# Pass change and last products of a down stage, and one turn in the attention stage: order and pages changed

## The reference, cut to what matters

```
u = rmsnorm(x);  proj = u @ w_in
ya, yb, yc = three attentions (A: 4 heads with two maps each; C: 8 heads; B: 8 heads, windowed)
h = x + rmsnorm((sum of sigmoid(gates) * (y @ w_proj)) @ w_out)
u = rmsnorm(h)
act = gelu(conv(u @ w_ffn_up)[:, :2816]) * conv(...)[:, 2816:]
out = h + rmsnorm(act @ w_ffn_down)          # 512x2816 @ 2816x1024
```

## Time and profile before

| | |
|---|---|
| median of 3 runs | 871.23 us |
| profiled execution's own time | 870.49 us |
| its span, first to last instruction | 868.7 us |
| mean granted TensorE clock | 0.995 |
| TensorE busy | 851.2 us, 98% |
| VectorE / ScalarE / GpSimd busy | 519.0 / 430.5 / 394.0 us |
| HBM read / written | 91.81 / 8.17 MB |

### The profile page before, as it was taken

The page is one execution under the profiler, slowest core; times in us unless marked ns, Lnnn a source line. Parts: engine busy times, 40 slices in busy tenths (PEclk is TensorE's granted clock), DMA queues, the critical chain, the costliest instruction groups (busy, mean ns, idle before and its releaser), DMA issues.

```text
span 868.7 us, 12772 instructions
## 1 busy us (share of the span) xinstructions
PE 851.2 (98%) x4182; PEld 715.1 (82%) x4182; DVE 519.0 (60%) x1050; ACT 430.5 (50%) x775; POOL 394.0 (45%) x542
## 2 busy tenths in 40 slices
PE   9999999999999999999999999999999999999877
PEld 7888887888888888888888889888888888888765
DVE  5677887888766733222222366555555555898884
ACT  6566666877666743333322526444444443454552
POOL 4554443234344447666666747555555554000001
PEclk9999999999999999999999999999999999999998
DMA  7541232322232223332328343333333333256472
GB/s 216 159 122 55 80 86 70 95 73 79 79 80 79 62 82 89 109 97 85 109 97 264 100 146 115 115 115 115 115 115 115 115 115 115 73 182 200 146 252 117
DMA packets 137617, 100.57 MB, mean 116 GB/s; under 512 B 7431, under 2 KB 122063, under 8 KB 137572
## 3 DMA queue, kind: packets, MB, share of 16 engines
q1 hardware_dynamic: 136666, 96.81, 36.6%
q10 hardware_dynamic: 906, 3.20, 1.0%
HBM read 91.81 MB, written 8.17 MB: 115 GB/s over the span
## 4 chain that ended last, share of the span: by engine, by line
PE 91%; DVE 4%; DMA 2%; issue 1%; POOL 1%; ACT 1%; SPq 1%; DVEq 0%; POOLq 0%; ACTq 0%
PE banks L1667 27%; PE banks L1669 26%; PE banks L1668 26%; PE banks L1838 2%; PE banks L1746 2%; PE banks L1747 2%; PE banks L1810 1%; DMA scratch<-second_tokens 1%; DMA ring_raw<-in_w_in_dram 1%; PE banks L1817 1%; DVE ring_lo L1593 1%; PE banks L1801 1%; DVE pages L1601 1%; PE banks L2016 1%; DVE scratch L1466 1%
## 5 line engine op out<-in xcount | busy, mean ns | idle before, releaser
L706 POOL TENSOR_TENSOR ring_lo<-ring_raw,ring_hi 128x256 fp32r<-128x256 f32 x472 | 357.9, 790 | 313.3 <-ACT ring_hi L818 313.2
L1667 PE MATMUL banks<-u_hi,ring_hi 128*128 128x512 f32 (+1 forms) x768 | 300.4, 391 | 0.2 <-DVE u_lo L1171 0.2
L1669 PE MATMUL banks<-u_hi,ring_lo 128*128 128x512 f32 (+1 forms) x768 | 296.0, 385 | 0.0
L1668 PE MATMUL banks<-u_lo,ring_hi 128*128 128x512 f32 (+1 forms) x768 | 295.6, 385 | 0.0
L1669 PEld LDWEIGHTS banks<-u_hi,ring_lo 128*128 128x128 f32 x768 | 144.3, 188 | 29.3
L1667 PEld LDWEIGHTS banks<-u_hi,ring_hi 128*128 128x128 f32 x768 | 144.4, 188 | 27.6 <-DVE u_lo L1171 0.4
L1668 PEld LDWEIGHTS banks<-u_lo,ring_hi 128*128 128x128 f32 x768 | 144.5, 188 | 27.3
L818 ACT CAST ring_hi<-ring_raw 128x1024 fp32r<-128x1024 f32 x118 | 122.8, 1043 | 61.2 <-PE banks L1669 54.2
L1507 DVE SCALAR_TENSOR_TENSOR wide<-banks,cols,wide 128x511 f32<-128x511 f32 x88 | 65.9, 749 | 96.4 <-ACT wide L1074 90.9
L1074 ACT ACTIVATE wide<-banks,cols 128x512 f32<-128x512 f32 x44 | 34.3, 778 | 98.0 <-PE banks L1669 98.0
L722 POOL TENSOR_SCALAR norm_ms<-norm_ss 128x1 f32<-128x1 f32 x15 | 2.9, 190 | 135.2 <-ACT pages L828 134.9
(11 more groups left out here) (217 smaller groups left out, 1337.3 us busy)
## 6 DMA issues: line engine op xcount, KB each, us to landing
ring_raw<-in_w_ffn_up_dram SPq DMA_DIRECT2D x88, 256.0 KB, 3.3
ring_raw<-in_w_in_dram SPq DMA_DIRECT2D x60, 256.0 KB, 3.4
ring_raw<-in_w_ffn_down_dram SPq DMA_DIRECT2D x55, 256.0 KB, 3.4
ring_raw<-in_w_gate_dram SPq DMA_DIRECT2D x48, 256.0 KB, 3.1
ring_raw<-in_w_out_dram SPq DMA_DIRECT2D x16, 256.0 KB, 2.9
second_tokens<-wide SPq DMA_DIRECT2D x10, 384.0 KB, 3.8
scratch<-second_tokens SPq DMA_DIRECT2D x10, 384.0 KB, 4.4
scratch<-in_x_dram SPq DMA_DIRECT2D x4, 512.0 KB, 5.9
```

What stands on the lines that cost most here:

```text
L706: last = pool.tensor_tensor(wlo[:, r, c], raw[:, r, c], whi[:, r, c].bitcast(F32), ALU.subtract)
L1667: pe.matmul(out, lhs_hi, rhs_hi, start=start, stop=False)
L1668: pe.matmul(out, lhs_hi, rhs_lo, start=False, stop=False)
L1669: return pe.matmul(out, lhs_lo, rhs_hi, start=False, stop=stop)
```

## The change

Four constants and orders change, in four places:

- `BY_TILE` 4 to 3 and `BY_PRODUCT` 3 to 2. In the last m, m3 of half 0 follows m2 of half 0 for each m.
- e21 of the two halves goes to pages of its own, `wide[:, 1, :]` and `scratch[:, 0, :]` (the first t4 page, free after its split). Both `make_e21` stand together, ahead of both `add_m5`. `split_second(1)` moves ahead of them on VectorE, and ahead of the copies back on ScalarE.
- SyncE issues the gain and all four residual rows after the last weight row and second tokens, gain first, then tiles 0, 2, 3, 1 (2 and 3 with a wait for `act2_lo` 9 and 10).
- In slot 18 `turn_y(3)` comes before the last projection step, and VectorE's `y_low_a(3)` before `results(17)`.

```diff
--- before.py
+++ after.py
@@ -67,7 +67,7 @@
 LAST_PAIR_AT = 6
 DOWN_SLOTS = (2, 3, 0)
 DOWN_ORDER = (0, 2, 3, 1)
-BY_TILE, BY_PRODUCT = 4, 3
+BY_TILE, BY_PRODUCT = 3, 2
 N_PAGES = 2 * FT
 
 SC_BANK, PT_BANK, O_BANK, G_BANK = 0, 2, 4, 6
@@ -302,7 +302,7 @@
         def kept_part(t):
             return raw[:, 1, 512 * t:512 * t + 512]
 
-        spare_part = wide[:, 1, :]
+        e21_parts = (wide[:, 1, :], scratch[:, 0, :])
         g_post_2 = xs_tmp
         spare_tmp = wide[:, 0:2, :].rearrange("p h n -> p (h n)")
 
@@ -671,13 +671,12 @@
                 load_down(FH + 3 + m)
                 if m + 2 < FH - 1:
                     load_second(m + 2)
-                if m == 6:
-                    sp.wait_ge(t4_lo, 7)
-                    for t in (0, 1):
-                        sp.dma_start(x_tok[:, t, :], h_dram[t]).then_inc(h_again[t], 16)
-                    sp.dma_start(g_post_2, g_post_ffn[0].partition_broadcast(P)).then_inc(gain_ffn_loaded, 16)
-            sp.wait_ge(act2_lo, FH - 1)
-            for t in (2, 3):
+            sp.wait_ge(t4_lo, 7)
+            sp.wait_ge(e21_back, 2)
+            sp.dma_start(g_post_2, g_post_ffn[0].partition_broadcast(P)).then_inc(gain_ffn_loaded, 16)
+            for t in DOWN_ORDER:
+                if t >= 2:
+                    sp.wait_ge(act2_lo, FH + t - 4)
                 sp.dma_start(x_tok[:, t, :], h_dram[t]).then_inc(h_again[t], 16)
             for i, t in enumerate(DOWN_ORDER[:-1]):
                 sp.wait_ge(h_done, TT + i + 1)
@@ -1138,10 +1137,11 @@
             act.wait_ge(t3_lo, FH)
             for t in range(2):
                 act.copy(kept_part(t), psum[:, M1_BANKS[t], :]).then_inc(m1_copied, 1)
-            for t, src in enumerate((spare_part, kept_part(0))):
+            split_second(1)
+            for t, src in enumerate(e21_parts):
                 act.wait_ge(e21_done, t + 1)
                 act.copy(psum[:, M7_BANKS[t], :], src).then_inc(e21_back, 1)
-            for m in range(1, FH):
+            for m in range(2, FH):
                 split_second(m)
             for i, t in enumerate(DOWN_ORDER[:-1]):
                 act.wait_ge(down_done, i + 1)
@@ -1405,12 +1405,14 @@
                     normed_heads(s - 1)
                     projections(s - 1)
                 softmax_out(s)
+                if s == 4 * TT + 2:
+                    y_low_a(u - 1)
                 if s >= 1:
                     results(s - 1)
                 if qt == 0 and u <= 8:
                     dve.wait_ge(v_hi, u + 1)
                     dve.tensor_tensor(v_parts(u)[1], turned_v(u), v_parts(u)[0].bitcast(F32), sub).then_inc(v_lo, 1)
-                if qt == 2 and 1 <= u <= 4:
+                if qt == 2 and 1 <= u < 4:
                     y_low_a(u - 1)
                 for g in range(3, T_ATT):
                     if FINISH[g] == s and projection_low_at_once(g):
@@ -1631,15 +1633,16 @@
             dve.wait_ge(m6_done, 1)
             keep_u2(0)
             keep_u2(1)
+            split_second(1)
             dve.wait_ge(m7_done, 1)
-            make_e21(0, spare_part)
+            dve.wait_ge(t4_lo, 1)
+            dve.wait_ge(down2_hi, 2)
+            for t in range(2):
+                make_e21(t, e21_parts[t])
             dve.wait_ge(m5_first, 1)
-            add_m5(0, spare_part)
-            dve.wait_ge(e12_done, 1)
-            make_e21(1, kept_part(0))
-            split_second(1)
+            add_m5(0, e21_parts[0])
             dve.wait_ge(down_used, FH)
-            add_m5(1, kept_part(0))
+            add_m5(1, e21_parts[1])
             for m in range(2, FH):
                 split_second(m)
 
@@ -1867,11 +1870,13 @@
             qk(0)
             for s in range(SLOTS):
                 u, qt = divmod(s, TT)
-                gemm_steps(STEPS[s])
+                first_steps = STEPS[s][:-1] if s == 4 * TT + 2 else STEPS[s]
+                gemm_steps(first_steps)
                 if qt == 0 and u <= 8:
                     turn_v(u)
                 if qt == 2 and 1 <= u <= 4:
                     turn_y(u - 1, s)
+                gemm_steps(STEPS[s][len(first_steps):])
                 if s >= 1:
                     pv(s - 1)
                 if s + 1 < SLOTS:
@@ -2108,7 +2113,6 @@
             for m in last:
                 second_ready(m)
                 m2(m, 0)
-            for m in last:
                 mm = m3(m, 0)
             mm.then_inc(down_done, 1)
             for t in range(2):
```

## The result

The changed kernel takes 859.34 us (median of 4 runs, 859.20 to 860.06) against 871.25 for the kernel before (4 runs, 871.17 to 871.50): 11.9 us less, a ratio of 0.9865 with a 95% interval of 0.9847 to 0.9882. Timed once more on another chip it took 859.75 against 870.55, 10.8 us less, ratio 0.9874 (0.9858 to 0.9890).

A forecast was written before the change was run, and what follows sets the result against it. TensorE, busy 98% of the span, was taken as the bound, leaving only its stalls and their clock loss to win. Terms -1.35 - 2.5 - 7.1 + 0.2 = -10.75 us took 871.23 to 860.5 us, range 859.5 to 862.8.

The forecast's parts named there:

- Slot 18: Attention stage, slot 18: turning earlier removes TensorE's stall before `turn_probs`; -1.35 us, bounds 0 and -1.44.
- The chain at the pass change: Start of pass 2: the copies back to TensorE end at 809.18, with pass 2's first matmul at 808.10.
- The pass change: Gap before m2 of m = 1: its split moves into pass 1's shadow, 2.62 us stall nearly goes; -2.5, bounds -2.6 and -0.6.
- the -7.1 of the end: Last m of pass 2: loads moved behind row 21 remove the waits and slow clock; -7.1 us, bounds -7.1 and -5.0.
- The median's distance: Whole kernel: the runs' median stays 0.74 us above the profiled execution, giving 860.5 us.
- best sum: Whole kernel: all terms at their favourable ends give 860.1 us.
- m3 behind m2: End of pass 2: m = 10's split has 2.8 us of margin; this order gives 6 of these steps.
- The tail: After tile 0's last product: a shorter last part makes VectorE the slower one; +0.2 us, bounds 0 and +0.8.
- rival 1: Pass change: the wait moves to the copy back, TensorE stands at m4(0); 862.5 us, chance 0.12.
- Rival 5: End of pass 2: the residual loads were not the reason and the wait stays; 867.6 us, chance 0.02.

The follow-up runs named there:

- the kernel before again: The kernel before, timed and profiled once more with no edit: 871.02 us (11 runs).
- slot 18 alone: The kernel before with only the reordering in slot 18: 869.95 us against 870.75, ratio 0.9988.
- the loads alone: The kernel before with only the gain and residual rows issued behind all weight rows: 866.16 us, ratio 0.9950.
- three m by tile alone: The kernel before with `BY_TILE` 3 instead of 4 and m3 of half 0 behind each m2, its other orders as before: 865.06 us, ratio 0.9936.
- the changed kernel without its pass change: The changed kernel with `BY_PRODUCT` 3 and the split of m = 1 last, as in the kernel before: 863.54 us against 859.75.
- the run with three k by product: The changed kernel with `BY_PRODUCT` 3 again, its new order of split and sums kept: 865.15 us, 5.4 slower than the changed kernel.
- four m by tile, all m2 first: The changed kernel with `BY_TILE` 4 and all m2 of half 0 ahead of all m3: 863.49 us, 3.7 slower than the changed kernel.

## Why the prediction was right and where it was wrong

The mechanism held in the main: TensorE stands nowhere in pass 2, as forecast. What failed are sizes, and part of the reason for the gain at the end.

**Slot 18: right.** 1.49 us in the trace for 1.35 forecast. From the first projection matmul to pass 2 the two profiles differ by 1.65 us.

**The chain at the pass change: right.** I put the end of the copies back 1.08 us after pass 2's first matmul; it is 1.07. The rows' pace of 0.60 us held: the rule of the Trainium skill ("VectorE: DVE Perf Modes", The DRAIN you can't avoid), that the next operation waits for the empty pipe, would have put it at 1.7 and made a stall of 0.5, of which there is none. I had applied it without the exception that the same section names, that an operation which is not held starts earlier; the traces show operations of 0.69 us that start 0.60 apart, as the exception allows.

**The pass change and the end, priced apart and from one execution: the step that failed.** "In the gap at the pass change it had stood 2.46 us and kept 2.4 GHz", and from that "I take -2.5", with -2.6 as the favourable bound. Of six profiles that have this wait of 2.45 us, the clock fell behind it in four (the kernel before again, slot 18 alone, the loads alone, three m by tile alone), to 1.2 GHz (granted clock 0.50) for about eight matmuls, 1.5 to 1.6 us each time. In two (the profile of before and the changed kernel without its pass change) it did not. So the place costs 2.7 to 2.8 us or 4.2 to 4.3, and taking the edit back out of the changed kernel cost 3.8 us in the medians, 1.3 more than the term.

The 1.3 can't simply be added to the sum, because the -7.1 of the end came from the same execution. Where the clock falls at the pass change, TensorE reaches the late rows later and waits less for them. The time above 198 steps in pass 2 was 2.8 and 7.1 us in the profile of before, 4.2 and 5.9 in the kernel before again, 4.3 and 5.6 in slot 18 alone: 9.8, 10.2 and 9.9 together, where my two terms make 9.6. The step that failed is the size of these two terms as a pair, 0.2 to 0.6 us too small, and the belief that each can be read off alone. On the profile that I predicted from, counted from the first projection matmul, the whole gain is 11.3 us for 10.75: the attention stage gave 0.3 more than its term and pass 2 0.2.

**The median's distance: the other step that failed.** "The median of the runs lies 0.74 above the profiled execution; I keep that distance". In the changed kernel the median lies 0.72 below the profiled execution (859.34 against 860.06), which started its first projection matmul 0.9 us later than that of before. With the start of before it would have taken 859.2 (an estimate, 860.06 less 0.90), and the median is 0.2 above that, not 0.74. This difference of 0.56 us and the 0.6 by which the terms were too small are nearly all of the 1.16 between 860.5 and 859.34. My range's lower end stood 0.6 below the best sum of one execution, while first projection matmuls start at 13.40 to 14.39 us in the traces, a spread of 1.0 us that no edit touches. On the second chip the gain was 10.8 us, within 0.1 of the forecast's 10.75, and on the first 11.9. The two intervals overlap, and the ratio that I forecast, 0.9877, lies inside both. I don't claim to know which of the two gains is the kernel's, and the agreement on the second chip doesn't show that the terms were right.

**The end: the size that of one execution, the cause half the story.** The 7.1 us that the profile of before lost there were all to be had, and TensorE ran 198 steps without a break; in two other profiles it was 5.9 and 5.6. The order of the loads ("After the change 1.5 MB of that stand behind") does make row 21 late: the longest landing of a weight row is 7.8 to 8.7 us in all six traces with the loads in front and 4.7 to 5.5 in all seven with them behind. But I gave them the whole gain, and counted m3 behind m2 as a margin. By the runs, the loads alone leave a 2.00 us wait at m = 10, and `BY_TILE` 3 with m3 behind m2 alone takes all of the end's waiting away with the loads untouched. With it in place, moving the loads is worth 0.5 us. The two edits each cover the same wait from its two sides, one by making the rows earlier, one by wanting them later. The parts alone gained 0.8, 4.6, 2.6 and 5.6 us, 13.6 in sum; together 10.8 on the same scale.

**The tail: right.** 0.14 us later at the last residual, and 0.17 from the last product to the end of the span (6.07 against 5.90), for 0.2 forecast.

**Rivals.** The copy back did not become a wait, but the run with three k by product shows that rival 1 was the real danger: the 3.65 us wait there is exactly its place. Rival 5 (the loads were not the reason) had 0.02 and was half true, only not with its consequence.

## What to carry to other kernels

Price a TensorE wait with two outcomes, its own length and its own length plus a slow stretch, and look at more than one execution before choosing. Where a later wait is for rows that come at a time of their own, it takes up what was lost before it: price the two together, and expect an edit at the first to be worth more once the second is mended (here 2.6 us alone, 3.8 with the end mended). For a wait on a supply chain, work out both when the data is ready and when it is wanted: reordering the consumer (want the last rows later) can be worth more than clearing the queue. And price each edit with the others in place and without them, since two that cover the same wait don't add up.

## What the runs showed of the hardware

- TensorE's clock fell to 1.2 GHz (granted clock 0.50, matmuls 0.43 us apart) behind waits of 2.45 us (in four of six) and of 2.00 us (four m by tile, all m2 first), and did not fall behind one of 2.00 us in the loads' run. The slow stretch may begin up to 1.5 us after TensorE has resumed.
- Loads of weight rows that were queued behind 1.5 MB of other loads took up to 7.8 to 8.7 us to land (six traces), and 4.7 to 5.5 at most without (seven traces); the median was 3.3 to 3.5 us either way.
- The slow transposes at the start are of different number in executions of one kernel. The pace of the warm-up transposes about doubles, from 4 or 5 in half a microsecond to 7, after some 10.5 us in the profile of before, 12 in the kernel before again and 13 in the changed kernel. The granted clock reads 1.00 all through this stretch, so the profile's clock column does not show the reason. The last 20 of them took 2.35 us in the profile of before, 2.43 in the kernel before again, 3.13 in the changed kernel:

```profile
11.41 2.43 PE L1694 MATMUL banks<-ident 128*128 128x128 f32 x20
13.99 0.39 PE L1667 MATMUL banks<-u_hi,ring_hi 128*128 128x256 f32 x1
```

```profile
11.42 3.13 PE L1697 MATMUL banks<-ident 128*128 128x128 f32 x20
14.30 0.36 PE L1670 MATMUL banks<-u_hi,ring_hi 128*128 128x256 f32 x1
```

  (the first fence is of the kernel before again, the second of the changed kernel). The Trainium skill ("TensorE: Matmul & The Clock Gate", What's actually happening) says that the number of slow matmuls at the start differs between runs of one kernel. The traces agree: the first projection matmul of the kernel before started at 13.40 us in one execution and at 13.99 in another.
